# Rows of the next expert transposed between the two halves of the down products

## The chip, the cores and the metric

The kernel runs on one core of one Trainium2 chip. The metric is the device time of one launch in microseconds (us). Three runs of the kernel before took 445.80, 446.79 and 448.35 us; their median, 446.79 us, is the time before.

## The reference

One step of a one-layer streaming encoder, all in fp32: a prompt of 512 rows and a sample of 64 rows, each row 1024 wide. A pooling mixer and differential attention come first, then a layer of 16 experts, and a last RMSNorm. What matters here is the layer of experts: a router gives each row two of 16 experts with weights, and each expert works on its rows.

```python
h2 = rmsnorm(x, g_ffn)
for e in range(N_EXPERTS):                                   # 16
    he = jax.nn.silu(h2 @ w_gate[e]) * (h2 @ w_up[e])        # 1024 -> 256
    moe = moe + combine[..., e:e+1] * (he @ w_down[e])       # 256 -> 1024
x = x + moe
```

## The kernel before

The program is written engine by engine, with semaphores between them; the order of every queue is the order in which the code is written. The first 250 us or so are the projections, the attention, the pooling, the output projection and the router. Then 16 experts follow one another; each takes up to 128 rows (a program branch for rows beyond that stands at the end).

For expert i, by engine:

- POOL gathers the rows of expert i by indirect DMA into `xg[i % 2]` (`gather_h2`, three experts ahead). It waits for the list of rows (`idx_ready`) and for the transposes that free the buffer (`xg_transposed`). It also gathers the sums so far (`gather_acc`) and stores results.
- SP loads three matrices of 1 MB for each expert into a ring of four slots.
- PE (TensorE) does for expert i, in `expert`: 32 gate and up products with 128 x 128 weights (`gate_up`, L1183; the trace shows two records of MATMUL for each of them, 64 in all); then the eight transposes of the rows of expert i + 1 (`transpose_rows`, L1177) into PSUM banks 0 and 1; then the lists of rows of expert i + 3 (`lists_of`, L1242, five small products, L1174); then the down products of expert i - 1 in two halves of 512 columns (`down_split`, L1198), six products each: two by two for the high and low parts of the weights (L1204, L1205), and two with the low part of the activations (L1209). Each half raises `down_done`.
- ACT (ScalarE) does the silu of expert i (L1595) when the gate products end, then eight copies of 128 columns (`rows_out`, L1574) that take the transposed rows of expert i + 1 out of PSUM into `xT`, scaled by `g_ffn`. The last copy raises `xT_act`, for which the gate products of expert i + 1 wait (L1249). Then it makes the high part of the down weights of expert i + 1 (`wd_his`, L1576), which waits for both halves of the down products of expert i - 1. From expert 6 on it also sums squares (L1601).
- DVE (VectorE) makes the product of silu and up (`he_out`), reads out the lists (`lists_out`), adds the down products to the sums (`add_rows`) when both halves are done, and makes the low part of the down weights (`wd_los`).

Experts 0 to 3 and 12 to 15 are written out, experts 4 to 11 are a loop of two turns. The parts of ACT and DVE are written out in full. The rows of experts 0 and 1 reach `xT` partly by DVE (`xT_dve`), and expert 0 has no down products beside it. The functions that the change touches, and what calls them:

Of the kernel before, what the change touches and what calls it, by code (L numbers as in the profile page):

```python
# [29 lines left out]
ALU = mybir.AluOpType  # L30
# [57 lines left out]
def build(nc, x_prompt, x_sample, cache_k, cache_v, state_pool, g_mix, w_in, w_pool, pool_scale,  # L88
# [4 lines left out]
    with ctx:  # L93
# [253 lines left out]
        lam_exp = sem("lam_exp")  # L347
        lam_made = sem("lam_made")
        lam_spread = sem("lam_spread")
# [48 lines left out]
        xT_dve = sem("xT_dve")  # L398
        xT_act = sem("xT_act")
        up_full = sem("up_full")  # L400
        gact_ready = sem("gact_ready")
# [184 lines left out]
        def _(pool):  # L586
# [45 lines left out]

            pool.wait_ge(lam_made, 1)
            pool.partition_broadcast(neglam[:, :], lam_t[0:1, 6:7]).then_inc(lam_spread, 1)
# [171 lines left out]
        def _(pe):  # L806
# [375 lines left out]

            def gate_up(slot, b, signal):  # L1183
                for w, first in ((wg_sb[slot], 0), (wu_sb[slot], FC)):
                    for c in range(FC):
                        for k in range(KC):
                            ins = pe.matmul(ps[:, 2 + b, (first + c) * P:(first + c + 1) * P], w[:, k, c * P:(c + 1) * P],  # L1187
                                            xT[:, b, k, :], start=(k == 0), stop=(k == KC - 1))
                ins.then_inc(signal, 1)
# [7 lines left out]

            def down_split(u, i, bank):  # L1198

                b, w_hi = u % 2, wd_hi(i if isinstance(i, int) else u)  # L1200
                for half in range(2):
                    n = slice(half * 512, (half + 1) * 512)
                    for c in range(FC):
                        pe.matmul(ps[:, bank + half, :], he_hi[:, b, c, :], w_hi[:, c, n], start=(c == 0), stop=False)  # L1204
                        pe.matmul(ps[:, bank + half, :], he_hi[:, b, c, :], wd_lo[u][:, c, n], start=False, stop=False)  # L1205
                    if half == 0:
                        pe.wait_ge(he_lo_ready, i + 1)
                    for c in range(FC):
                        ins = pe.matmul(ps[:, bank + half, :], he_lo[:, b, c, :], w_hi[:, c, n], start=False, stop=(c == FC - 1))  # L1209
                    ins.then_inc(down_done, 1)  # L1210

            def first_rows():
# [23 lines left out]
            def expert(it, u, left):  # L1236
# [9 lines left out]

                if isinstance(it, int) and i <= 1:
                    pe.wait_ge(xT_dve, i + 1)
                pe.wait_ge(xT_act, i + 1)  # L1249
                pe.wait_ge(ring_loaded[u], it * 48 + 48)  # L1250
                gate_up(u, b, up_full)
                if isinstance(it, int) and i == 1:
                    for n in (1, 2):
                        lists_of(n)
                if left is None or left >= 1:
                    pe.wait_ge(xg_loaded[1 - b], it * (8 * RING) + 16 * ((u + 1) // 2 + 1))
                    transpose_rows(1 - b, xg_transposed)
                if first:
                    pe.wait_ge(tab_ready, 1)
                    for n in range(2):  # L1260
# [3 lines left out]
                if not first and left != 0:  # L1264
# [3 lines left out]
                    pe.wait_ge(wd_lo_ready, i)  # L1268
                    down_split((u - 1) % RING, i - 1, 4)
                if left == 1:  # L1270
# [45 lines left out]
        def _(act):  # L1316
# [287 lines left out]
            for i in range(E):  # L1604
# [5 lines left out]
                if i + 1 < E:  # L1610
                    act.wait_ge(xg_transposed, i + 2)
                    for k in range(4 if i == 0 else 0, KC):
                        ins = rows_out((i + 1) % 2, k)
                    ins.then_inc(xT_act, 1)
                    if i < E - 2:
# [28 lines left out]
        def _(dve):  # L1644
# [132 lines left out]
            step(dve.tensor_tensor(lam_t[:, 4:5], lam_t[:, 3:4], lam_t[:, 2:3], ALU.subtract))  # L1777
            dve.tensor_scalar(lam_t[:, 6:7], lam_t[:, 4:5], -LAMBDA_INIT, None, ALU.add).then_inc(lam_made, 1)
            w_in_los(3)
# [535 lines left out]
```

## Time and profile before

| | |
|---|---|
| three runs, median | 446.79 us (445.80 to 448.35) |
| the profiled execution, its own time | 445.62 us |
| its span, first to last instruction | 443.2 us |
| PE busy | 417.2 us (94%) |
| DVE, ACT, POOL busy | 273.6, 197.6, 125.0 us |
| mean granted TensorE clock | 0.985 |

The profile is of one execution. Start times count from the span's start. A record of a matmul overlaps the next one (they are pipelined), so distances of starts tell the pace, and the length of a single record does not. PEld is the weight load, which runs ahead of its matmul. The idle time in brackets is the engine's own just before the record, with what ended it.

### The profile page before, as it was taken

How to read it: one execution, taken by the hardware profiler on the slowest of the kernel's cores; microseconds unless marked ns; L12 is line 12 of the kernel's file. 1: busy time of each engine (PE TensorE's matmuls, PEld its weight loads, DVE VectorE, ACT ScalarE, POOL GpSimd, SP SyncE). 2: the span in 40 equal slices, each digit the busy share in tenths (PEclk: the TensorE clock that was granted, in tenths of full speed). 3: DMA queues.
4: the chain of work that ended last, by engine and by line, in shares of the span. 5: the costliest groups of instructions: out<-in, count | busy, mean ns of one | idle time of the engine just before them, and what ended most of it. 6: DMA issues, size and time to landing. Idle time of an engine off the chain costs nothing.

```text
span 443.2 us, 7774 instructions
## 1 busy us (share of the span) xinstructions
PE 417.2 (94%) x2926; PEld 365.2 (82%) x2927; DVE 273.6 (62%) x655; ACT 197.6 (45%) x485; POOL 125.0 (28%) x207
## 2 busy tenths in 40 slices
PE   7899999999999999999998998999999999999970
PEld 3786999997777777788895988999999999989950
DVE  3855231707779888464258897555577777569770
ACT  6475321605666755232124433444555555447340
POOL 2010000200143407250001304333345555355331
PEclk9999999999999999999998999999999999999995
DMA  8851705306000069814126599999999999973220
GB/s 280 295 164 48 226 1 167 130 1 198 2 1 3 1 266 378 328 53 163 78 95 247 172 405 389 363 363 352 362 352 361 355 350 382 351 274 129 57 78 21
DMA packets 32073, 91.36 MB, mean 206 GB/s; under 512 B 11200, under 2 KB 11712, under 8 KB 27942
## 3 DMA queue, kind: packets, MB, share of 16 engines
q1 hardware_dynamic: 20790, 71.97, 43.9%
q0 software_dynamic: 11248, 18.93, 12.0%
q8 instruction: 21, 0.34, 0.3%
q14 instruction: 14, 0.11, 0.1%
HBM read 86.38 MB, written 26.01 MB: 254 GB/s over the span
## 4 chain that ended last, share of the span: by engine, by line
PE 64%; DVE 16%; DMA 7%; issue 6%; ACT 4%; POOL 0%; POOLq 0%; SPq 0%; DVEq 0%; ACTq 0%
PE ps L1187 13%; PE ps L822 10%; PE ps L824 9%; PE ps L823 9%; DMA region_x<-h_rows,lists 5%; PE ps L978 2%; PE ps L1204 2%; PE ps L1205 2%; PE ps L1209 2%; PE ps L1124 2%; PE ps L943 2%; PE ps L1180 1%; DMA region_w<-in_w_in 1%; DMA out_y_sample<-region_x,lists 1%; PE ps L961 1%
## 5 line engine op out<-in xcount | busy, mean ns | idle before, releaser
L1187 PEld LDWEIGHTS ps<-region_p,region_a 128*128 128x128 f32 x512 | 58.3, 192 | 1.7 <-DVE region_p L2024 1.1
L1187 PE MATMUL ps<-region_p,region_a 128*128 128x128 f32 x512 | 58.5, 275 | 0.7 <-DVE region_p L2024 0.7
L824 PE MATMUL ps<-region_a_r,region_w_r 128*128 128x288 f32 x192 | 56.5, 294 | 0.0
L822 PE MATMUL ps<-region_a_r,ring_r 128*128 128x288 f32 x128 | 40.5, 317 | 0.0
L823 PE MATMUL ps<-region_a_r,ring_r 128*128 128x288 f32 x128 | 37.7, 295 | 0.0
L824 PEld LDWEIGHTS ps<-region_a_r,region_w_r 128*128 128x128 f32 x192 | 36.0, 188 | 0.0
L1574 ACT ACTIVATE region_p<-ps,gffn_sb 128x128 f32<-128x128 f32 x116 | 31.6, 383 | 8.5 <-PE ps L1180 6.7
L1595 ACT ACTIVATE region_t<-ps 128x256 f32<-128x256 f32 x16 | 6.1, 384 | 55.9 <-PE ps L1187 43.7
L699 POOL DMA_INDIRECT region_x<-h_rows,lists x13 | 16.6, 1280 | 48.6 <-DVE slot_w L2122 48.2
L1187 PEld LDWEIGHTS ps<-region_p,ring 128*128 128x128 f32 x256 | 29.1, 192 | 0.8 <-DVE region_p L2046 0.5
L1187 PE MATMUL ps<-region_p,ring 128*128 128x128 f32 x256 | 29.3, 275 | 0.4 <-DVE region_p L2046 0.4
L822 PEld LDWEIGHTS ps<-region_a_r,ring_r 128*128 128x128 f32 x128 | 24.0, 188 | 6.9 <-issue 3.3
L1187 PEld LDWEIGHTS ps<-region_p,region_w 128*128 128x128 f32 x256 | 29.2, 192 | 0.3
L1187 PE MATMUL ps<-region_p,region_w 128*128 128x128 f32 x256 | 29.2, 275 | 0.0
L1761 DVE TENSOR_SCALAR region_q<-ps 128x288 f32<-128x288 f32 x8 | 3.7, 458 | 39.8 <-PE ps L824 39.8
L2128 DVE TENSOR_TENSOR region_t_r<-region_t,ps 128x256 fp32r<-128x256 f32 x16 | 6.7, 419 | 33.8 <-ACT region_t L1595 24.3
L2145 DVE SCALAR_TENSOR_TENSOR mix<-ps,slot_w,mix 128x1024 f32<-128x1024 f32 x15 | 19.2, 1282 | 11.1 <-PE ps L1209 6.2
L823 PE MATMUL ps<-region_w_r,mix_r 128*128 128x512 f32 x64 | 25.0, 390 | 0.0
L1204 PE MATMUL ps<-region_q_r,region_t_r 128*128 128x512 f32 x60 | 24.7, 411 | 0.0
L823 PEld LDWEIGHTS ps<-region_a_r,ring_r 128*128 128x128 f32 x128 | 24.1, 188 | 0.0
L1437 ACT ACTIVATE region_p<-ps,negm 128x128 f32<-128x128 f32 (+4 forms) x40 | 20.7, 527 | 5.8 <-DVE negm L1793 5.8
L704 POOL DMA_INDIRECT out_y_prompt<-region_x,lists x12 | 12.0, 1002 | 35.8 <-DVE region_x L2161 32.7
(358 smaller groups left out, 1024.9 us busy)
## 6 DMA issues: line engine op xcount, KB each, us to landing
region_a<-in_w_gate SPq DMA_DIRECT2D x8, 1024.0 KB
region_a<-in_w_up SPq DMA_DIRECT2D x8, 1024.0 KB
region_a<-in_w_down SPq DMA_DIRECT2D x8, 1024.0 KB
region_w<-in_w_in SPq DMA_DIRECT2D x2, 2048.0 KB, 10.3
region_w<-in_w_out SPq DMA_DIRECT2D x2, 2048.0 KB, 8.0
ring<-in_w_gate SPq DMA_DIRECT2D x4, 1024.0 KB
ring<-in_w_up SPq DMA_DIRECT2D x4, 1024.0 KB
ring<-in_w_down SPq DMA_DIRECT2D x4, 1024.0 KB
```

The source lines that it names most:

```text
L699: pool.indirect_dma_start(out=dst, out_offset=None, in_=src, in_offset=bass.IndirectOffsetOnAxis(ap=at, axis=0), bounds_check=bound[n], oo ...
L704: pool.indirect_dma_start(out=dst, out_offset=bass.IndirectOffsetOnAxis(ap=at, axis=0), in_=src, in_offset=None, bounds_check=bound[n], oo ...
L822: pe.matmul(out, lhs_hi, rhs_hi, start=first, stop=False)
L823: pe.matmul(out, lhs_hi, rhs_lo, start=False, stop=False)
L824: return pe.matmul(out, lhs_lo, rhs_hi, start=False, stop=last)
L943: ins = pe.matmul(ps[:, b + c, 0:(t + 1) * P], q, kT[r, h, 0:(t + 1) * P], start=True, stop=True)
L978: ins = pe.matmul(ps[0:m, O_BANK[t], h * VD:(h + 1) * VD], aT[0:keys, n % 2, k * P:k * P + m], v, start=(k == 0), stop=(k == len(tiles) - 1))
L1187: ins = pe.matmul(ps[:, 2 + b, (first + c) * P:(first + c + 1) * P], w[:, k, c * P:(c + 1) * P], xT[:, b, k, :], start=(k == 0), stop=(k = ...
L1204: pe.matmul(ps[:, bank + half, :], he_hi[:, b, c, :], w_hi[:, c, n], start=(c == 0), stop=False)
L1437: ins = act.activation(prob[0:m, n % 2, c, 0:w], ps[0:m, 2 * (n % 2) + c, 0:w], ACT.Exp, bias=negm[0:m, n % 2, c:c + 1], scale=-1.0, accum ...
L1574: return act.activation(xT[:, b, k, :], ps[:, k // 4, (k % 4) * P:(k % 4 + 1) * P], ACT.Copy, scale=gffn_sb[:, k:k + 1])
L2145: dve.scalar_tensor_tensor(acc, ps[:, bank:bank + 2, :], slot_w[:, w:w + 1], acc, ALU.mult, ALU.add).then_inc(added, 1)
```

## The change

The transposes of the rows of expert i + 1 move from in front of the lists to between the two halves of the down products of expert i - 1 (for experts 1 to 14; expert 0, which has no down products, keeps its order). ACT's eight copies raise a new semaphore, `xT_half`, after the fourth, and `xT_act` after the eighth as before. From expert 2 on the gate products wait for `xT_half` at the first product, and for `xT_act` at the fifth (k = 4 of the first group of eight). The semaphore `lam_made` is dropped: its one signal goes to `lam_dots`, and its waiter on POOL waits for the second count of that.

```diff
@@ -345,7 +345,6 @@
         hist_evac = sem("hist_evac")
         lam_dots = sem("lam_dots")
         lam_exp = sem("lam_exp")
-        lam_made = sem("lam_made")
         lam_spread = sem("lam_spread")
         scores_full = sem("scores_full")
         negm_ready = sem("negm_ready")
@@ -397,6 +396,7 @@
         xg_transposed = sem("xg_transposed")
         xT_dve = sem("xT_dve")
         xT_act = sem("xT_act")
+        xT_half = sem("xT_half")
         up_full = sem("up_full")
         gact_ready = sem("gact_ready")
         he_ready = sem("he_ready")
@@ -630,7 +630,7 @@
                 pool.wait_ge(ktok_evac, t + 1)
                 pool.dma_start(kp_v[t] if t < PT else ks_v, k_st[0:rows(t), t, :]).then_inc(k_stored, 16)
 
-            pool.wait_ge(lam_made, 1)
+            pool.wait_ge(lam_dots, 2)
             pool.partition_broadcast(neglam[:, :], lam_t[0:1, 6:7]).then_inc(lam_spread, 1)
 
 
@@ -1180,10 +1180,12 @@
                     ins = pe.transpose(ps[:, k // 4, (k % 4) * P:(k % 4 + 1) * P], src[:, k, :], ident[:, :])
                 ins.then_inc(signal, 1)
 
-            def gate_up(slot, b, signal):
+            def gate_up(slot, b, signal, rest=None):
                 for w, first in ((wg_sb[slot], 0), (wu_sb[slot], FC)):
                     for c in range(FC):
                         for k in range(KC):
+                            if rest is not None and first == 0 and c == 0 and k == KC // 2:
+                                pe.wait_ge(xT_act, rest)
                             ins = pe.matmul(ps[:, 2 + b, (first + c) * P:(first + c + 1) * P], w[:, k, c * P:(c + 1) * P],
                                             xT[:, b, k, :], start=(k == 0), stop=(k == KC - 1))
                 ins.then_inc(signal, 1)
@@ -1195,7 +1197,7 @@
                                         start=(c == 0), stop=(c == FC - 1))
                 ins.then_inc(signal, 1)
 
-            def down_split(u, i, bank):
+            def down_split(u, i, bank, between=None):
 
                 b, w_hi = u % 2, wd_hi(i if isinstance(i, int) else u)
                 for half in range(2):
@@ -1208,6 +1210,8 @@
                     for c in range(FC):
                         ins = pe.matmul(ps[:, bank + half, :], he_lo[:, b, c, :], w_hi[:, c, n], start=False, stop=(c == FC - 1))
                     ins.then_inc(down_done, 1)
+                    if half == 0 and between is not None:
+                        between()
 
             def first_rows():
 
@@ -1244,18 +1248,24 @@
                     pe.wait_ge(idx_ready, i + n + EARLY + (1 if first and n == 0 else 0))
                     slot_lists((u + n) % RING * EPG + it + (u + n) // RING, (u + n) % RING)
 
-                if isinstance(it, int) and i <= 1:
+                early = isinstance(it, int) and i <= 1
+                if early:
                     pe.wait_ge(xT_dve, i + 1)
-                pe.wait_ge(xT_act, i + 1)
+                    pe.wait_ge(xT_act, i + 1)
+                else:
+                    pe.wait_ge(xT_half, i - 1)
                 pe.wait_ge(ring_loaded[u], it * 48 + 48)
-                gate_up(u, b, up_full)
+                gate_up(u, b, up_full, None if early else i + 1)
                 if isinstance(it, int) and i == 1:
                     for n in (1, 2):
                         lists_of(n)
-                if left is None or left >= 1:
+
+                def next_rows():
                     pe.wait_ge(xg_loaded[1 - b], it * (8 * RING) + 16 * ((u + 1) // 2 + 1))
                     transpose_rows(1 - b, xg_transposed)
+
                 if first:
+                    next_rows()
                     pe.wait_ge(tab_ready, 1)
                     for n in range(2):
                         lists_of(n)
@@ -1266,7 +1276,7 @@
                     if not (isinstance(it, int) and i == 1):
                         pe.wait_ge(added, i - 1)
                     pe.wait_ge(wd_lo_ready, i)
-                    down_split((u - 1) % RING, i - 1, 4)
+                    down_split((u - 1) % RING, i - 1, 4, next_rows)
                 if left == 1:
                     pe.wait_ge(idx_ready, E + EARLY + 1)
                     pe.wait_ge(he_ready, i + 1)
@@ -1611,6 +1621,8 @@
                     act.wait_ge(xg_transposed, i + 2)
                     for k in range(4 if i == 0 else 0, KC):
                         ins = rows_out((i + 1) % 2, k)
+                        if i >= 1 and k == KC // 2 - 1:
+                            ins.then_inc(xT_half, 1)
                     ins.then_inc(xT_act, 1)
                     if i < E - 2:
                         wd_his(i + 1)
@@ -1775,7 +1787,7 @@
             dve.tensor_copy(histT[:, :, :], ps[:, 3, 0:H * HIST].rearrange("p (g s) -> p g s", g=H)).then_inc(hist_evac, 1)
             dve.wait_ge(lam_exp, 1)
             step(dve.tensor_tensor(lam_t[:, 4:5], lam_t[:, 3:4], lam_t[:, 2:3], ALU.subtract))
-            dve.tensor_scalar(lam_t[:, 6:7], lam_t[:, 4:5], -LAMBDA_INIT, None, ALU.add).then_inc(lam_made, 1)
+            dve.tensor_scalar(lam_t[:, 6:7], lam_t[:, 4:5], -LAMBDA_INIT, None, ALU.add).then_inc(lam_dots, 1)
             w_in_los(3)
             for j in range(H + 1, 2 * H):
                 head_out(j)
```

On PE, expert 2's turn (the later turns repeat it), the order before, from the end of the gate products (L1187) over the transposes (L1180), the lists (L1174) and the first half of the down products (L1204, L1205, L1209):

```order
L1187 MATMUL ps<-region_p,region_a 128x128 x31
L1180 MATMUL ps<-ident,region_x 128x128 [waits xg_loaded1]
L1180 MATMUL ps<-ident,region_x 128x128 x7
L1174 MATMUL ps<-region_q,region_v 128x8 [waits idx_ready,onehot_ready]
L1174 MATMUL ps<-region_q,region_v 128x8 x4
L1204 MATMUL ps<-region_q_r,region_t_r 128x512 [waits wd_lo_ready,added,he_ready]
L1205 MATMUL ps<-region_a_r,region_t_r 128x512
L1204 MATMUL ps<-region_q_r,region_t_r 128x512
L1205 MATMUL ps<-region_a_r,region_t_r 128x512
L1209 MATMUL ps<-region_q_r,region_t_r 128x512 [waits he_lo_ready]
L1209 MATMUL ps<-region_q_r,region_t_r 128x512
```

and now, from the end of that first half (L1211 here) to the fifth gate product of the next expert (L1189):

```order
L1211 MATMUL ps<-region_q_r,region_t_r 128x512 [waits he_lo_ready]
L1211 MATMUL ps<-region_q_r,region_t_r 128x512
L1180 MATMUL ps<-ident,region_x 128x128 [waits xg_loaded1]
L1180 MATMUL ps<-ident,region_x 128x128 x7
L1206 MATMUL ps<-region_q_r,region_t_r 128x512
L1207 MATMUL ps<-region_a_r,region_t_r 128x512
L1206 MATMUL ps<-region_q_r,region_t_r 128x512
L1207 MATMUL ps<-region_a_r,region_t_r 128x512
L1211 MATMUL ps<-region_q_r,region_t_r 128x512 x2
L1189 MATMUL ps<-region_p,region_w 128x128 [waits ring_loaded3,xT_half]
L1189 MATMUL ps<-region_p,region_w 128x128 x3
L1189 MATMUL ps<-region_p,region_w 128x128 [waits xT_act]
```

The transposes stand behind six of the twelve down products instead of in front of all of them and of the lists; six products are left between them and the next expert's gate products, whose one wait has become two.

On PE, expert 1, the first with down products: before, the transposes stood ahead of the third group of lists, which waits for `idx_ready`.

```order
L1174 MATMUL ps<-region_q,region_v 128x8 [waits idx_ready,onehot_ready]
L1174 MATMUL ps<-region_q,region_v 128x8 x4
L1180 MATMUL ps<-ident,region_x 128x128 [waits xg_loaded0]
L1180 MATMUL ps<-ident,region_x 128x128 x7
L1174 MATMUL ps<-region_q,region_v 128x8 [waits idx_ready,onehot_ready]
L1174 MATMUL ps<-region_q,region_v 128x8 x4
L1204 MATMUL ps<-region_q_r,region_t_r 128x512 [waits wd_lo_ready,he_ready]
```

Now the lists and the first half come first.

```order
L1174 MATMUL ps<-region_q,region_v 128x8 [waits idx_ready,onehot_ready]
L1174 MATMUL ps<-region_q,region_v 128x8 x4
L1174 MATMUL ps<-region_q,region_v 128x8 [waits idx_ready,onehot_ready]
L1174 MATMUL ps<-region_q,region_v 128x8 x4
L1206 MATMUL ps<-region_q_r,region_t_r 128x512 [waits wd_lo_ready,he_ready]
L1207 MATMUL ps<-ring_r,region_t_r 128x512
L1206 MATMUL ps<-region_q_r,region_t_r 128x512
L1207 MATMUL ps<-ring_r,region_t_r 128x512
L1211 MATMUL ps<-region_q_r,region_t_r 128x512 [waits he_lo_ready]
L1211 MATMUL ps<-region_q_r,region_t_r 128x512
L1180 MATMUL ps<-ident,region_x 128x128 [waits xg_loaded0]
L1180 MATMUL ps<-ident,region_x 128x128 x7
```

The wait for `idx_ready` now has nothing of the transposes in front of it. The order of ACT's, DVE's and POOL's instructions is as before.

## Rows read from the trace of the kernel before

**Rows 1.** The page: busy time of PE and ACT, and the granted clock by slices.

```profile
PE 417.2 (94%) x2926; PEld 365.2 (82%) x2927; DVE 273.6 (62%) x655; ACT 197.6 (45%) x485; POOL 125.0 (28%) x207
...
PEclk9999999999999999999998999999999999999995
```

**Rows 2.** Stretches: length, busy of PE, PEld, DVE, ACT, POOL, granted clock, DMA share, GB/s.

```profile
304.50:315.50 11.00, 11.00 (x92) 10.49 (x91) 5.67 (x9) 4.55 (x11) 4.09 (x3) 1.00 0.95 363
...
381.50:393.60 12.10, 11.06 (x90) 10.37 (x90) 8.47 (x23) 5.55 (x13) 6.02 (x6) 1.00 0.85 332
```

**Rows 3.** Waits of PE over the whole span: total us, times, longest.

```profile
PE ps L1174 <- DVE slot_w L2122: 1.5, 1, 1.5
...
PE ps L1180 <- DMA region_x<-h_rows,lists: 1.0, 1, 1.0
```

**Rows 4.** The chain that ended last, in order of time: start, us.

```profile
368.70 20.81 DMA region_x<-h_rows,lists
389.56 1.09 PE ps L1180 x8
```

**Rows 5.** Timeline of PE and PEld, expert 5's turn: start, us, line.

```profile
311.50 1.04 PE L1180 MATMUL ps<-ident,region_x 128*128 128x128 f32 x8
...
312.37 0.27 PE L1174 MATMUL ps<-region_q,region_v 128*128 x5
...
312.50 0.47 PE L1204 MATMUL ps<-region_q_r,region_t_r 128*128 128x512 f32 x1
...
313.97 0.39 PE L1204 MATMUL ps<-region_q_r,region_t_r 128*128 128x512 f32 x1
...
315.11 7.34 PEld L1187 LDWEIGHTS ps<-region_p,region_a 128*128 128x128 f32 x64
315.34 7.30 PE L1187 MATMUL ps<-region_p,region_a 128*128 128x128 f32 x64
```

**Rows 6.** Timeline of ACT, same turn, cut after four copies, then whole.

```profile
312.57 1.14 ACT L1574 ACTIVATE region_p<-ps,gffn_sb 128x128 f32<-128x128 f32 x4 [0.49 <-PE ps L1180]
...
312.57 2.17 ACT L1574 ACTIVATE region_p<-ps,gffn_sb 128x128 f32<-128x128 f32 x8 [0.49 <-PE ps L1180]
315.59 1.99 ACT L1588 CAST region_q_r<-region_a 128x1024 fp32r<-128x1024 f32 x2 [0.84 <-PE ps L1209]
```

**Rows 7.** Timeline, a gate start after a wait (expert 1), its second record; a start without.

```profile
257.62 0.69 DVE L2024 TENSOR_TENSOR region_p<-ps,gffn_sb 128x512 f32<-128x512 f32 x1
...
258.36 0.38 PE L1187 MATMUL ps<-region_p,region_a 128*128 128x128 f32 x1 [0.65 <-DVE region_p L2024]
...
258.57 0.50 PE L1187 MATMUL ps<-region_p,region_a 128*128 128x128 f32 x3
...
315.44 0.39 PE L1187 MATMUL ps<-region_p,region_a 128*128 128x128 f32 x2
```

**Rows 8.** Timeline of PE, expert 1's turn.

```profile
265.86 1.07 PE L1180 MATMUL ps<-ident,region_x 128*128 128x128 f32 x8
268.41 0.27 PE L1174 MATMUL ps<-region_q,region_v 128*128 128x8 bf16 x5 [1.48 <-DVE slot_w L2122]
```

**Rows 9.** Timeline of DVE and POOL, the gather three experts ahead, expert 5's turn.

```profile
313.38 0.15 DVE L2122 TENSOR_REDUCE slot_w<-ps 128x1 f32<-128x3 f32 x1
...
313.80 1.33 POOL L699 DMA_INDIRECT region_x<-h_rows,lists  x1 [4.62 <-DVE slot_w L2122]
```

**Rows 10.** Timeline of DVE, the low part of the down weights, expert 7's turn.

```profile
340.31 2.35 DVE L2135 TENSOR_TENSOR ring_r<-ring,region_q_r 128x1024 fp32r<-128x1024 f32 x2
```

**Rows 11.** Timeline of PE: expert 12's gate, expert 14's turn, expert 15's gate.

```profile
381.22 7.30 PE L1187 MATMUL ps<-region_p,ring 128*128 128x128 f32 x64
...
411.34 1.04 PE L1180 MATMUL ps<-ident,region_x 128*128 128x128 f32 x8
...
417.67 2.50 PE L1187 MATMUL ps<-region_p,region_w 128*128 128x128 f32 x21
```

**Rows 12.** The page's group of ACT's copies: count, busy us, mean ns of one.

```profile
L1574 ACT ACTIVATE region_p<-ps,gffn_sb 128x128 f32<-128x128 f32 x116 | 31.6, 383 | 8.5 <-PE ps L1180 6.7
```

## Prediction

> **What bounds the kernel now.** I read the page first: PE is busy for 417.2 of 443.2 us, and its granted clock is full in nearly every slice [rows 1]. Then the stretches: from 271 us on each expert takes one turn of 11.0 us in which PE has no idle time at all, while DMA is 0.95 busy and ACT only 4.55 us [rows 2]. So in the expert stage anything put on PE, or any wait of PE, is paid in full; work of ACT is free as long as PE doesn't wait for it. The waits of PE name two of interest: 1.5 us for the lists in expert 1's turn and 1.0 us for gathered rows [rows 3]. The chain shows the second: a gather issued at 368.70 landed 20.81 us later, and the transposes started at 389.56 [rows 4]. Expert 12's gate products had started at 381.22 [rows 11]; in an undisturbed turn the transposes follow a gate's start after 7.14 us (64 records, 0.11 us apart, 7.30 us with the last one's tail [rows 5]), so they were wanted at 388.36. This late gather costs 1.20 us, which the turn of 12.10 us confirms [rows 2]. It is all that the move of the transposes can win in this execution.
>
> **What the move does in an ordinary turn.** Transposes, lists and down products take the same time in another order. In [rows 5] the eight transposes take 312.37 - 311.50 = 0.87 us, the lists 0.13, the first half 313.97 - 312.50 = 1.47 and the second half 315.34 - 313.97 = 1.37. Before, ACT's copies had the lists and both halves as cover, 2.97 us. Now they have the second half alone, 1.37 us.
>
> Count from S, the start of the transposes. The gate products of the next expert are wanted at S + 0.87 + 1.37 = S + 2.24. ACT starts copying at S + 1.07 (312.57 against 311.50), has four copies at + 1.14 and eight at + 2.17 [rows 6]; ACT is idle before the copies in this row, so nothing in its queue makes them later. The two signals thus fall at S + 2.21 and S + 3.24. From a signal to PE takes 0.05 us: DVE ends at 258.31 and the waiting matmul starts at 258.36 [rows 7].
>
> - First product: possible at S + 2.26, wanted at S + 2.24. But its weight load otherwise runs 0.23 us ahead, under the last down product (315.11 against 315.34 [rows 5]), and can't before the signal. A gate that starts from a wait has its second record 0.21 us after the first (258.57), one that doesn't 0.10 (315.44) [rows 7]. So 0.02 + 0.11 = 0.13 us are lost.
> - Fifth product, the ninth record: wanted 8 x 0.111 = 0.89 us after the first, at S + 3.13; possible at S + 3.29, thus 0.16 late, and 0.11 for the load that isn't ahead: 0.27 us. The first loss is inside this one, since PE would get there at S + 3.26, still before the signal.
>
> So each gate start loses **0.27 us**. This holds for experts 2 to 14, 13 of them; expert 15's gate has expert 14's down products in front too (transposes at 411.34, gate at 417.67 [rows 11]) and waits for nothing. 13 x 0.27 = 3.5 us. Bounds: 13 x 0.16 = 2.1 if the late load costs nothing, 13 x (0.13 + 0.27) = 5.2 if the two losses add.
>
> **A price by the Trainium skill.** By the Trainium skill (ScalarE: Activation LUTs, Rules for kernel authors) an ACTIVATE costs about 0.3 us and 0.83 ns for each element, an estimate of 0.41 us for 128 columns and 3.25 for eight; each gate would wait 1.08 us more, and my forecast would become 463 us. The trace disagrees: eight of them end in 2.17 us [rows 6].
>
> **Expert 1's turn.** PE reached the end of its lists at 265.86, did the transposes, and then stood until 268.41 for the lists from DVE [rows 8]; the 0.87 us of transposes lay in that wait. Now the wait comes first and is ended by the same DVE record, and the transposes come behind it, uncovered: **+0.87 us**. The gate loss after it is among the 13.
>
> **The late gather.** The gather three experts ahead is issued 0.27 us after the lists are read out (313.38 + 0.15, then 313.80 [rows 9]), but POOL also waits for the transposes that free the buffer. These now start 0.13 + 1.47 = 1.60 us later, are seen done at S + 1.07 = 314.17, and the gather goes out at 314.2 to 314.4, some 0.5 us later than now. It is wanted 1.60 us later, and two gate losses (0.54) lie between. The time left from issue to need grows from 388.36 - 368.70 = 19.66 us to 21.3; it took 20.8 to land. So the wait should go: **-1.20 us**, and the weights, which share the DMA engines, get 2% longer turns. Its bounds are 0 and -1.20 in this execution.
>
> **What costs nothing.** ACT makes the next down weights' high part behind the copies, now from S + 3.24, 1.0 us after the gate was due instead of 0.25 [rows 5, 6]. It takes 2.0 us, so both parts stand 3.0 us after the gate's start. DVE begins the low part at 340.31 [rows 10], 3.0 us after that turn's gate (two turns of 11.0 us after 315.34), and needs one part at a time. That cover is a whole turn deep, since PE wants the result a turn later. The end of the second half, which frees weights for SP and sums for DVE, keeps its place. `lam_made` into `lam_dots` moves one signal between the same two instructions: 0. The register instructions for the added wait run ahead on PE's sequencer: 0, at most hundredths in the loop.
>
> **The sum.** 445.62 (the profiled execution) + 0.87 + 3.5 - 1.20 = 448.8 us. This execution lies 1.17 us under the median of the three runs, 446.79, and no row tells what the others lose. I carry half of that, 0.6, over: **449.4 us**.
>
> **The rivals.** About 0.5%, 2.2 us, is what a measurement of this kernel can tell: faster is below 444.6, slower above 449.0.
>
> 1. *Late gathers cost more in ordinary runs.* The three runs spread over 2.55 us while PE's work is fixed, and DMA is near full [rows 2], so gathers are what can differ. If all of the 1.17 us is theirs, the change takes 2.4 us away; with the lower bound of the gate loss, 446.79 + 0.87 + 2.1 - 2.4 = 447.4 us. Against it: the profile has one late gather in 13 turns. Within 0.5%.
> 2. *The gates don't wait.* The second half of the down products hides the copies after all; it decides whether the signals reach PE before S + 2.01 and S + 3.02, some 0.25 us earlier than I find. Then 445.62 + 0.87 - 1.20 = 445.3 us, and if expert 1's transposes find another cover, 444.4. For it: the margin is a quarter of a microsecond, and the ends of records are modelled for matmuls. Against it: ACT's start 1.07 us behind the first transpose is measured, and so are its copies.
> 3. *Both losses add, and the gather stays late*, since it is issued later too: 445.62 + 0.87 + 5.2 + 0.6 = 452.3 us.
> 4. *The copies don't overlap.* One takes 383 ns [rows 12]; end to end eight take 3.06 us instead of 2.17, and 13 gates lose 0.89 more: 461 us. In the trace they overlap in every turn. The Trainium skill's price above would be a case of this.
>
> That the change does not do what it says can be left out: the order of PE's queue shows both waits and the new place.
>
> **How the numbers follow.** My case 0.54 (0.49 slower, 0.05 within); rival 1 0.20, within; rival 2 0.14 (0.06 within, 0.08 faster); rival 3 0.08 and rival 4 0.02, slower; anything else that makes it faster 0.02. Together: faster 0.10, within 0.5% 0.31, slower 0.59. The range goes from rival 1 with a little of rival 2, 446.8, to just under rival 3, 452.0. My case alone has 447.4 (2.1 for the gates, median not carried) to 451.1 (5.2, half carried).
>
> **What would show it.** In the changed profile: turns of 11.25 to 11.30 us instead of 11.0, with 0.2 to 0.3 us of idle time of PE at the first and fifth gate product, ended by ACT's copies (L1584); the second ACT group of a turn starting 1.0 us after the gate's due time; no wait for gathered rows at expert 12; expert 1's gate to expert 2's gate longer by 0.9 to 1.2 us. Turns of 11.0 us would prove the gate loss wrong, and turns above 11.5 us would mean the copies come later than S + 1.07. If a wait for gathered rows stays, the 1.20 us are wrong.

## The result: 450.29 against 446.76 us

The changed kernel takes 450.29 us (median of 20 runs, 447.75 to 451.89), the kernel before 446.76 (20 runs, 445.15 to 448.38): a ratio of 1.008, interval 1.0065 to 1.0095. It is slower, by more than the 0.5% that the prediction set as its bound. (Ratios here and below are those on record with their 95% intervals; they can differ by up to 0.15% from the quotient of the two medians beside them.) The forecast was 449.4, the range 446.8 to 452.0.

The profiled execution took 450.57 us, with a span of 448.7. The page's busy times of it answer to [rows 1]; PE has 4.8 us more and still the same share:

```profile
PE 422.0 (94%) x2926; PEld 365.6 (81%) x2927; DVE 274.1 (61%) x655; ACT 196.2 (44%) x485; POOL 119.1 (27%) x207
```

The waits of PE (first line) and of its weight loads (second line) over the whole span, us in total, times and longest, answer to [rows 3]:

```profile
PE ps L1174 <- DVE slot_w L2134: 2.4, 1, 2.4
...
PEld ps L1189 <- ACT region_p L1584: 3.0, 11, 0.3
```

The wait for the lists has grown from 1.5 to 2.4 us, the wait for gathered rows is not in the answer any more, and weight loads of the gate products now wait for ACT's copies, 0.3 us at most.

Expert 5's turn in the timeline (start, us, instruction, idle time before it and what ended it) answers to [rows 5, 6, 9]:

```profile
317.51 1.03 PE L1180 MATMUL ps<-ident,region_x 128*128 128x128 f32 x8
318.30 0.48 PE L1206 MATMUL ps<-region_q_r,region_t_r 128*128 128x512 f32 x1
318.58 2.17 ACT L1584 ACTIVATE region_p<-ps,gffn_sb 128x128 f32<-128x128 f32 x8 [2.08 <-PE ps L1180]
319.30 0.99 POOL L699 DMA_INDIRECT region_x<-h_rows,lists  x1 [6.67 <-PE ps L1180]
319.77 6.35 PEld L1189 LDWEIGHTS ps<-region_p,region_a 128*128 128x128 f32 x55 [0.28 <-ACT region_p L1584]
319.77 7.55 PE L1189 MATMUL ps<-region_p,region_a 128*128 128x128 f32 x64
320.60 2.04 ACT L1598 CAST region_q_r<-region_a 128x1024 fp32r<-128x1024 f32 x2
320.81 0.19 PEld L1189 LDWEIGHTS ps<-region_p,region_a 128*128 128x128 f32 x1
328.76 1.04 PE L1180 MATMUL ps<-ident,region_x 128*128 128x128 f32 x8
```

With S = 317.51, the start of the transposes, the copies start at S + 1.07 and take 2.17 us as before, the first gate load goes at S + 2.26 and the fifth product's (the one at 320.81) at S + 3.30. The 64 gate records take 7.55 us instead of 7.30: the loss appears as longer records, not as idle time of PE. From S to the next S it is 11.25 us.

Where the 5.5 us between the two spans (443.2 and 448.7 us) went, by the first gate record of an expert (expert 1 and expert 15, the same products as in [rows 7, 11]):

| | expert 1's gate | expert 15's gate | between | from there to the end |
|---|---|---|---|---|
| before | 258.36 | 417.67 | 159.31 | 25.55 |
| after | 260.85 | 423.32 | 162.47 | 25.38 |

So 3.16 us arose between these two gates, 2.49 before expert 1, and -0.17 behind. (The executions' own times differ by 4.95 us; 0.5 us less of the later one lies outside the span.) The three terms of the sum, 0.87 + 3.5 - 1.20, make 3.17.

### The profile page after: what moved, and what is told of

It reads as the page before. It is cut to its first block, busy times and chain, and to the rows that moved or that the text cites. A ratio compares the mean times of both kernels' runs of the same rounds, so it can differ in the third digit from the quotient of the medians.

```text
span 448.7 us, 7774 instructions
## 1 busy us (share of the span) xinstructions
PE 422.0 (94%) x2926; PEld 365.6 (81%) x2927; DVE 274.1 (61%) x655; ACT 196.2 (44%) x485; POOL 119.1 (27%) x207
## 4 chain that ended last, share of the span: by engine, by line
PE 79%; DVE 10%; ACT 4%; issue 3%; DMA 1%; POOLq 0%; POOL 0%; SPq 0%; DVEq 0%; ACTq 0%
PE ps L1189 23%; PE ps L822 10%; PE ps L824 9%; PE ps L823 9%; PE ps L1206 3%; PE ps L1207 3%; PE ps L1211 3%; PE ps L1180 3%; PE ps L978 2%; PE ps L1124 2%; PE ps L943 2%; DMA region_x<-in_x_prompt 1%; PE ps L961 1%; PE ps L1111 1%; PE ps L818 1%
## 5 line engine op out<-in xcount | busy, mean ns | idle before, releaser
L1189 PEld LDWEIGHTS ps<-region_p,region_a 128*128 128x128 f32 x512 | 58.3, 192 | 3.5 <-ACT region_p L1584 1.9
L1189 PE MATMUL ps<-region_p,region_a 128*128 128x128 f32 x512 | 60.3, 278 | 0.7 <-DVE region_p L2036 0.7
L699 POOL DMA_INDIRECT region_x<-h_rows,lists x13 | 12.9, 995 | 66.0 <-PE ps L1180 51.5
L1189 PEld LDWEIGHTS ps<-region_p,ring 128*128 128x128 f32 x256 | 29.1, 192 | 1.6 <-issue 0.7
L1189 PE MATMUL ps<-region_p,ring 128*128 128x128 f32 x256 | 29.9, 278 | 0.4 <-DVE region_p L2058 0.4
L1189 PEld LDWEIGHTS ps<-region_p,region_w 128*128 128x128 f32 x256 | 29.2, 192 | 1.1 <-ACT region_p L1584 0.8
L1189 PE MATMUL ps<-region_p,region_w 128*128 128x128 f32 x256 | 30.0, 277 | 0.0
L1206 PE MATMUL ps<-region_q_r,region_t_r 128*128 128x512 f32 x60 | 25.9, 432 | 0.0
L2157 DVE SCALAR_TENSOR_TENSOR mix<-ps,slot_w,mix 128x1024 f32<-128x1024 f32 x15 | 19.2, 1281 | 10.5 <-PE ps L1211 7.1
L1447 ACT ACTIVATE region_p<-ps,negm 128x128 f32<-128x128 f32 (+4 forms) x40 | 20.7, 527 | 5.8 <-DVE negm L1805 5.8
L1542 ACT ACTIVATE region_v<-region_q 128x512 f32<-128x512 f32 (+1 forms) x10 | 6.3, 627 | 32.7 <-DVE region_q L1912 19.5
```

What stands on the lines that cost most here:

```text
L699: pool.indirect_dma_start(out=dst, out_offset=None, in_=src, in_offset=bass.IndirectOffsetOnAxis(ap=at, axis=0), bounds_check=bound[n], oo ...
L1447: ins = act.activation(prob[0:m, n % 2, c, 0:w], ps[0:m, 2 * (n % 2) + c, 0:w], ACT.Exp, bias=negm[0:m, n % 2, c:c + 1], scale=-1.0, accum ...
L2157: dve.scalar_tensor_tensor(acc, ps[:, bank:bank + 2, :], slot_w[:, w:w + 1], acc, ALU.mult, ALU.add).then_inc(added, 1)
```

## The experiments

The theory: each ordinary turn loses 0.27 us because ACT's copies lost 1.6 us of their cover, expert 1's turn loses 0.87 us of transposes that lay in a wait, and 1.20 us of a late gather come back. The rivals that matter now: the second wait costs by itself, the turns are longer for another cause, and the gather was punctual by chance.

"Stage" below is the time from expert 1's first gate record to expert 15's, 159.31 before and 162.47 with the change.

### Both signals, transposes at their old place

```diff
-                if first:
+                if left is None or left >= 1:
                     next_rows()
+                if first:
...
-                    down_split((u - 1) % RING, i - 1, 4, next_rows)
+                    down_split((u - 1) % RING, i - 1, 4)
```

> The transposes go back in front of the lists, in every turn; the two signals and the two waits of the gate products stay. Theory (the gate products wait because the copies have too little cover behind the transposes): with the lists and both halves as cover again, neither wait is ever open, turns are 11.0 us, and the time is that of the kernel before, 446.8 +- 0.7 us, ratio 1.000. Rival (the added wait itself, its instructions in PE's queue or the weight load it holds back, costs the 0.27 us a turn): turns stay at 11.25 us, and the time is 446.8 + 13 x 0.27 = 450.3 us, ratio 1.008.

Measured: 446.37 against 446.81 us, ratio 0.9996 (0.9975 to 1.0017); stage 158.91. Turns are 10.98 us and no weight load waits for ACT's copies. The wait for rows is here too. PE's timeline, two ordinary turns and expert 12's:

```profile
312.57 1.04 PE L1180 MATMUL ps<-ident,region_x 128*128 128x128 f32 x8
...
323.55 1.04 PE L1180 MATMUL ps<-ident,region_x 128*128 128x128 f32 x8
...
390.25 0.98 PE L1180 MATMUL ps<-ident,region_x 128*128 128x128 f32 x7 [0.66 <-DMA region_x<-h_rows,lists]
```

Two signals in place of one cost nothing as long as both are early, so the whole loss of the ordinary turns comes with the place; and the late gather returns with the old place.

### The new place with one signal

```diff
...
-                    pe.wait_ge(xT_half, i - 1)
+                    pe.wait_ge(xT_act, i + 1)
                 pe.wait_ge(ring_loaded[u], it * 48 + 48)
-                gate_up(u, b, up_full, None if early else i + 1)
+                gate_up(u, b, up_full)
...
```

Left out above: `xT_half` itself and ACT's raising of it, which go too.

> The transposes stay between the halves; the gate products wait once, at the first product, for all eight copies. Theory: the first product can start 3.24 + 0.05 us after the first transpose, is wanted at 2.24, and its load costs 0.11 more, so a turn loses 1.16 us instead of 0.27: turns of 12.1 us, and 450.3 + 13 x 0.89 = 461.9 us, ratio 1.034. Rival (the loss of 0.27 us is that of transposes amid the down products, not of waits for the copies): turns of 11.25 us and 450.3 us, ratio 1.008.

Measured: 460.46 against 446.81 (461.9 was forecast), ratio 1.031 (1.0281 to 1.0339); stage 175.71, turns of 12.14 us. The waits of PE, and one gate of its timeline:

```profile
PE ps L1188 <- ACT region_p L1583: 11.6, 13, 1.0
...
322.35 0.82 PE L1188 MATMUL ps<-region_p,region_a 128*128 128x128 f32 x5 [0.89 <-ACT region_p L1583]
```

All 13 gates wait for the eighth copy, 0.9 us in the mean. This is the predicted mechanism without its remedy: the cover of 1.37 us against copies that stand at S + 3.24. The split signal gets 0.9 us of each 1.16 back. The turn of expert 1 showed something else, told further down.

### The change, with expert 1's transposes at their old place

```diff
-                if first:
+                if early:
                     next_rows()
+                if first:
...
-                    down_split((u - 1) % RING, i - 1, 4, next_rows)
+                    down_split((u - 1) % RING, i - 1, 4, None if early else next_rows)
```

> As the change, but in expert 1's turn the transposes stand where they stood before, ahead of the lists for which PE waits there. Theory: the 0.87 us of expert 1's transposes are hidden in that wait again, and expert 2's gate does not wait (0.27): 450.3 - 1.14 = 449.2 us, ratio 1.005; the later turns stay at 11.25 us. Rival (that stretch is paced by DVE, and PE's order there is worth nothing): 450.3 us, and expert 2's gate starts as late as in the change.

Measured: 448.33 against 446.81 (449.2 was forecast), ratio 1.0045 (1.0026 to 1.0064); stage 161.39, 1.08 less than with the whole change. The timelines of PE, the changed kernel first:

```profile
260.85 1.38 PE L1189 MATMUL ps<-region_p,region_a 128*128 128x128 f32 x10 [0.66 <-DVE region_p L2036]
...
270.89 0.27 PE L1174 MATMUL ps<-region_q,region_v 128*128 128x8 bf16 x5 [2.40 <-DVE slot_w L2134]
272.49 1.04 PE L1180 MATMUL ps<-ident,region_x 128*128 128x128 f32 x8
274.76 0.49 PE L1189 MATMUL ps<-region_p,region_a 128*128 128x128 f32 x2
```

and this one:

```profile
259.21 7.41 PE L1189 MATMUL ps<-region_p,region_a 128*128 128x128 f32 x64 [0.67 <-DVE region_p L2037]
...
266.71 1.07 PE L1180 MATMUL ps<-ident,region_x 128*128 128x128 f32 x8
269.26 0.27 PE L1174 MATMUL ps<-region_q,region_v 128*128 128x8 bf16 x5 [1.48 <-DVE slot_w L2135]
272.25 0.94 PE L1189 MATMUL ps<-region_p,region_a 128*128 128x128 f32 x7
```

From gate to gate, expert 1's turn is 13.91 us with the change (274.76 - 260.85) and 13.04 here (272.25 - 259.21), as before the change: 0.87 us. With the gate loss of expert 2, which goes too, 1.14 were expected of the stage. By the two ratios this kernel is 1.6 us below the change, with intervals wide enough for 1.1.

### Transposes behind four of the twelve down products

```diff
                     if half == 0:
+                        if between is not None:
+                            between()
                         pe.wait_ge(he_lo_ready, i + 1)
...
-                    if half == 0 and between is not None:
-                        between()
```

> As the change, but the transposes stand behind four of the twelve down products instead of six, so that eight of them cover the copies: 0.87 + 8 x 0.228 = 2.69 us from the first transpose to the gate instead of 2.24. Theory: the first load is wanted at 2.46, the signal reaches it at 2.26; the fifth is wanted at 3.47, its signal is there at 3.29; no gate waits, turns are 11.0 us, and the time is 450.3 - 3.5 = 446.8 us, ratio 1.000; expert 1's 0.87 us stay, and the late gather of expert 12's turn comes back at most in part, since the transposes stand 1.1 us later than before. Rival (transposes amid the down products cost 0.27 us a turn wherever they stand): 450.3 us, ratio 1.008, turns of 11.25 us.

Measured: 446.65 against 446.81 (446.8 was forecast), ratio 0.9999 (0.9985 to 1.0013). Eight products now cover the copies, and the turns are 11.0 us; the gate loss is gone. But the stage is 160.89, for expert 1's turn took 15.5 us. Stretches of this kernel (length, busy of PE, PEld, DVE, ACT and POOL, granted clock, DMA share, GB/s), the first two in that turn:

```profile
265.00:269.31 4.31, 1.91 (x25) 1.60 (x24) 3.97 (x20) 0.38 (x1) 0.99 (x1) 1.00 1.01 414
269.31:272.72 3.41, 3.41 (x13) 2.93 (x12) 0.61 (x1) 2.17 (x8) 0.98 (x1) 0.50 1.01 424
273.26:284.26 11.00, 11.00 (x90) 10.44 (x89) 5.66 (x9) 4.02 (x10) 3.17 (x3) 1.00 0.88 323
```

For 3.41 us the granted clock was 0.50, the 1.2 GHz level. PE had stood 2.40 us for the lists until 267.81. The third stretch is an ordinary turn. The gathered rows only just came in time; the waits of the weight loads have them twice:

```profile
PEld ps L1180 <- DMA region_x<-h_rows,lists: 0.6, 2, 0.4
```

At expert 12 PE lost next to nothing by it, at expert 13 the transposes started about 0.1 us late.

### Both edits together

The diffs of the last two kernels (expert 1's transposes at their old place, and four of the twelve down products in front of the others) in one: the later place, without the gate loss and without the loss of expert 1's turn.

> The two edits together: transposes behind four of the twelve down products from expert 2 on, and in expert 1's turn where they stood before. Theory: no gate waits (3.5 us back), expert 1's 0.87 us are hidden again, and PE does not stand for 2.4 us in one piece in that turn, after which two of four profiles with the transposes behind the lists show a granted clock of 0.50 for 3.4 us (some 1.5 us, in about half of the executions: 0.8): 450.3 - 3.5 - 0.87 - 0.8 = 445.1 us, ratio 0.996, turns of 11.0 us, no clock of 0.50 in expert 1's turn. Rival (the gains overlap, since DVE paces that stretch): 446.6 us as with four products alone, ratio 1.000.

Measured: 445.94 against 445.95, ratio 0.9999 (0.9981 to 1.0018); stage 159.36, nothing gained. Turns are 11.0 us and expert 1's is 13.01, as wanted. The 0.87 and 3.5 us should be gone, and with the gather's 1.20 kept the stage should be 158.1 us (159.31 - 1.20). The missing part is in the turn from expert 13's gate to expert 14's, 11.96 us long (10.76 before), in the timelines of PE and DVE:

```profile
393.76 7.30 PE L1189 MATMUL ps<-region_p,region_a 128*128 128x128 f32 x64
...
399.98 1.28 DVE L2158 SCALAR_TENSOR_TENSOR mix<-ps,slot_w,mix 128x1024 f32<-128x1024 f32 x1 [2.92 <-DMA mix<-summed_rows,lists]
401.36 0.47 PE L1206 MATMUL ps<-region_q_r,region_t_r 128*128 128x512 f32 x1 [0.30 <-issue]
402.94 1.09 PE L1180 MATMUL ps<-ident,region_x 128*128 128x128 f32 x8 [0.41 <-DMA region_x<-h_rows,lists]
...
405.72 7.31 PE L1189 MATMUL ps<-region_p,region_a 128*128 128x128 f32 x64
```

PE stood 0.41 us for gathered rows here, and 0.30 us just before that because of gathered sums: DVE waited 2.92 us for them, and the down products, which need DVE's result, started 0.1 us after it. (The profile names no releaser for this wait, it says "issue"; the cause is read from the times.) By starts the two delays are longer than the idle time, since a record's tail covers part of it: the down products start 7.60 us after the gate, against 7.07 in the same turn of the kernel with four products. So the later place alone doesn't make the gathers punctual.

### Half of the copies on DVE

```diff
-                    for k in range(4 if i == 0 else 0, KC):
+                    for k in range(4, KC):
...
+                if i >= 1:
+                    dve.wait_ge(xg_transposed, i + 2)
+                    rows_out((i + 1) % 2).then_inc(xT_dve, 1)
```

The gate products' first wait is for `xT_dve` instead of `xT_half`; place and expert 1 as in the kernel with expert 1's transposes at their old place.

> Transposes between the halves as in the change (in expert 1's turn where they stood before), but DVE copies the first four blocks in one instruction of 0.69 us while ACT copies the last four in 1.14 us. Theory: the first product's rows are ready 1.2 + 0.69 = 1.9 us after the first transpose, its load is wanted at 2.01; ACT's are ready at 2.21, wanted at 2.9. So no gate waits though the transposes stand where the change put them, turns are 11.0 us, the late gather is gone, and the time is 445.1 us, ratio 0.996. Rival (the place between the halves costs in itself): turns of 11.25 us, 448.3 us as with expert 1 put back alone. A third outcome: DVE is held up by its own queue in the later turns and the gates wait for it, turns above 11.0 us from expert 6 on.

Measured: 446.20 against 445.95, ratio 1.001 (0.9988 to 1.0032); stage 160.28. Again the ordinary turns are 11.0 us, so the place between the halves costs nothing by itself; and again gathers come late, rows in expert 12's turn and sums in expert 13's, by the timelines of PE and DVE:

```profile
390.46 1.09 PE L1179 MATMUL ps<-ident,region_x 128*128 128x128 f32 x8 [0.38 <-DMA region_x<-h_rows,lists]
...
399.44 1.28 DVE L2153 SCALAR_TENSOR_TENSOR mix<-ps,slot_w,mix 128x1024 f32<-128x1024 f32 x1 [3.09 <-DMA mix<-summed_rows,lists]
400.83 0.47 PE L1205 MATMUL ps<-region_q_r,region_t_r 128*128 128x512 f32 x1 [0.74 <-issue]
```

A second way to remove the gate loss ends as the first: this kernel and the one with both edits were each forecast at 445.1 us, which takes the late gather to be gone, and both missed that.

### Longer turns at the old place

The kernel before, with one spare product in front of each gate from expert 2 on; the output doesn't depend on it.

```diff
                 pe.wait_ge(ring_loaded[u], it * 48 + 48)
+                if not (isinstance(it, int) and i <= 1):
+                    keep_running(1, 2 + b)
                 gate_up(u, b, up_full)
```

> The kernel before, order and waits untouched, with one spare product of 512 columns (0.215 us) in front of each expert's gate products from expert 2 on; it is no part of the result. Turns become 11.2 us, as long as the change's but for 0.05. Question: what took the late gather away in the changed kernel. Theory of the prediction (the later place of the transposes, 1.6 us more until the rows are wanted): here the place is the old one, so PE still waits for gathered rows at expert 12, 0.5 us or more, and the time is 446.0 + 14 x 0.215 - at most 0.7 = 448.3 to 449.0 us. Rival (longer turns let the DMA engines, 0.95 busy, catch up, and any slack on PE's side is eaten by them): no wait for gathered rows on PE, and 446.0 + 3.0 - 1.0 = 448.0 us or less.

Measured: 447.64 against 446.25, ratio 1.0029 (1.0008 to 1.005); stage 161.91, turns of 11.2 us. PE's timeline:

```profile
402.71 1.09 PE L1180 MATMUL ps<-ident,region_x 128*128 128x128 f32 x8 [0.51 <-DMA region_x<-h_rows,lists]
```

Longer turns alone push the wait one expert later and shrink it to 0.51 us, but don't remove it. Neither expectation came out as written: the time is the rival's (448.0 or less), but the wait that the rival excluded is there; the theory has the wait, but at expert 12 and with 448.3 us or more.

### Spare products in expert 1's wait, twice, beside the change again

To keep PE busy in the wait after which the clock had fallen: the changed kernel and ten spare products of 512 columns, whose results nobody reads.

```diff
                 if isinstance(it, int) and i == 1:
                     for n in (1, 2):
                         lists_of(n)
+                    keep_running(10, 4)
```

> As the change, but in expert 1's turn PE runs ten spare products of 512 columns (2.15 us at full clock) into an unused bank after the second group of lists, where it would otherwise stand for 2.4 us. They are no part of the result. Theory (that idle stretch lets the granted clock fall to 0.50 in about half of the executions, which costs some 1.5 us each time): no clock of 0.50 there, and 450.3 - 0.8 = 449.5 us, ratio 1.006. Rival (the clock there is worth nothing in the mean, and the change costs 3.5 us by its waits and expert 1's transposes alone): 450.3 us, ratio 1.008. If the spare products run into the signal, expert 2's gate starts later than 13.9 us after expert 1's.

> The changed kernel once more, beside the next one on the same chip, for a second profile. Theory (PE's idle 2.4 us in expert 1's turn lets the granted clock fall in some executions): 450 us, ratio 1.008; turns of 11.25 us; a clock of 0.50 in expert 1's turn as likely as not. Rival: never a clock of 0.50 there with this order.

> The kernel with the spare products in expert 1's wait, beside the changed kernel on the same chip. Theory: no clock of 0.50 in expert 1's turn, 0.5 to 0.8 us less than the changed kernel in the median. Rival: the same time as the changed kernel within 0.3 us.

Measured: 449.07 (ratio 1.0073, 1.0045 to 1.01) and again 449.32 (1.0076, 1.0047 to 1.0106); the changed kernel beside the second, 449.55 (1.0089, 1.0056 to 1.0122). Their stages are 162.47, 162.55 and 162.52. The products filled the wait, by PE's timeline of the first of them:

```profile
266.86 2.32 PE L880 MATMUL ps<-ones 128*128 128x512 bf16 x10
269.40 0.27 PE L1174 MATMUL ps<-region_q,region_v 128*128 128x8 bf16 x5 [0.23 <-DVE slot_w L2135]
```

The intervals overlap, and the stretch over expert 1's turn of the changed kernel's second profile has the full clock:

```profile
268.00:274.90 6.90, 4.49 (x39) 3.69 (x37) 4.74 (x20) 1.54 (x6) 1.43 (x2) 1.00 1.00 421
```

So the low clock in expert 1's turn is no main part of the change's loss. Whether it takes some tenths of the median stays open. The count "two of four" in an expectation above was one profile too high when it was written; with this profile it is right: of four profiles with 2.4 us of idle time there, two fell to 0.50 and two, both of the changed kernel itself, did not.

## Why the prediction was right

- **What the move does in an ordinary turn** held to a hundredth. The signals were to reach the first load at S + 2.26 and the fifth product's at S + 3.29; the records say S + 2.26 and S + 3.30, and the turn is 11.25 us. The cause was the copies' cover: with two signals and the old place nothing was lost, with eight products as cover, or half of the copies on DVE, the turns went back to 11.0. "Idle time of PE at the first and fifth gate product" was not to be seen as such: PE has no such wait in its list. It is the weight load of the first product that stood for ACT, 0.28 us by the row of 319.77; at the fifth, too little to be listed, and what is lost lies in the longer records.
- **Expert 1's turn** held: 0.87 us, measured by undoing that part alone.
- **The late gather** held in what came of it: no wait for rows in the two profiles of the change, the two with spare products and the one with expert 1 undone, and turns of 11.25 and 11.04 us around expert 12. Its working was 0.6 us off. These are, in the changed kernel, the gather that expert 12's turn needs and the transposes that need it:

```profile
375.58 1.00 POOL L699 DMA_INDIRECT region_x<-h_rows,lists  x1 [3.13 <-PE ps L1180]
...
396.26 0.93 PE L1180 MATMUL ps<-ident,region_x 128*128 128x128 f32 x7
```

  From issue to need are 20.7 us, not 21.3, because POOL issues the gather at S + 1.8 (319.30 for S = 317.51 above) and not at S + 1.1 to 1.3. With the 20.8 us of [rows 4] it would still have been 0.1 late; it landed after 20.0. The same two times in all profiles with turns of 11.0 to 11.25 us, for the same expert's rows (us; where PE waited, the need is when it would have started):

| | issue to need | issue to landing |
|---|---|---|
| before; both signals at the old place | 19.7; 19.7 | 20.8; 20.4 |
| longer turns at the old place | 20.1 | 19.7 |
| four products; both edits; half on DVE | 20.2; 20.2; 20.2 | 20.1; 19.8; 20.7 |
| the change, twice | 20.7; 20.7 | 20.0; 20.4 |
| with spare products, twice; expert 1 undone | 20.7; 20.7; 20.7 | 19.2; 19.9; 19.4 |

  The left column is the prediction's mechanism: the later place gives 0.5 us, and two gate losses give 0.5 more. The right column varies by 1.6 us from profile to profile, and no row tells why. So the five punctual gathers follow from the place and the gate losses together, but with margins of 0.3 to 1.5 us against that variation there was luck in it that none was late. The kernels without the loss had a wait for rows of 0.4 us (both edits at expert 13, half on DVE at expert 12) or a start just in time (four products). The 1.20 us thus came back in full only in kernels that had the gate loss.
- **What costs nothing** held. The casts started at 320.60, 0.85 us after the gate was due (1.0 forecast), and no gate waited for weights.
- **The sum** came to 448.8 for an execution like the one profiled before; the one profiled after had 450.57. The weak step is "I carry half of that, 0.6, over". No row said that the change gives the other half back, and it did not: the medians differ by 3.53 us, the terms make 3.17, and added to the whole median they would have given 446.79 + 3.17 = 450.0 us. What differed between the two executions beside the terms arose in the first 20 us: expert 0's gate starts at 250.58 instead of 248.09, which is 2.49 us, as much as at expert 1's. Stretches of both from 13.20 to 16.50, the changed kernel first:

```profile
13.20:16.50 3.30, 3.30 (x12) 2.71 (x12) 0.89 (x3) 0.00 (x0) 0.00 (x0) 0.50 0.89 323
```

```profile
13.20:16.50 3.30, 3.30 (x20) 2.87 (x19) 1.49 (x4) 2.07 (x4) 0.00 (x0) 1.00 0.97 301
```

  The clock was at half in the one and full in the other, with 12 records of PE instead of 20. Ahead of that the one was late by 0.88 us, by the timelines, again the changed kernel first:

```profile
11.19 0.73 PE L835 MATMUL ps<-mix_r,region_a_r 128*128 128x512 f32 x2 [1.13 <-ACT region_a_r L1356]
```

```profile
10.31 0.73 PE L835 MATMUL ps<-mix_r,region_a_r 128*128 128x512 f32 x2 [0.20 <-ACT region_a_r L1346]
```

  The second profile of the change has this low clock too, at 13.57 to 16.98, though the order of PE's instructions there is as before the change; no other profile has it, and as long a wait at this line (1.3 us with both edits together) went without. Whether that is chance stays open. Against its being in most runs of the change speaks that these were only 0.23 us above the kernel with spare products, in whose profile expert 0's gate started 1.43 us earlier (249.27 against 250.70).
- **The rivals.** *Late gathers cost more in ordinary runs* fell: no gather was late in the changed kernel's profiles, and the loss was over 0.5%. *The gates don't wait* fell: they do, in each turn. *Both losses add, and the gather stays late* fell on both points. *The copies don't overlap* fell: eight take 2.17 us again, and with it the 463 us that came of adding up eight whole prices of the Trainium skill (ScalarE: Activation LUTs, Rules for kernel authors).

No version beat the kernel before by a measurable amount.

## What to carry to other kernels

When a producer is moved later in an engine's queue, count from its end to its consumer what is left as cover for the engine between them; here 1.37 us of cover against 2.17 us of copies, and a signal in two parts paid for most of the gap but not all. A wait that work was hidden in is a resource: before moving that work, look where the wait will stand. And when a second resource is nearly full, a gain on the first may depend on the first being slow: undo the loss and see whether the gain stays. A forecast that hangs on half a microsecond between two times of 20 needs the spread of both, and one profile doesn't give it.

## What the runs showed of the hardware

- After PE had stood idle for 2.40 to 2.42 us in expert 1's turn, the granted clock was 0.50 for 3.4 us in two of four profiles. One of them stands above; the other is the new place with one signal:

```profile
267.26:270.68 3.42, 3.35 (x14) 2.70 (x15) 2.14 (x8) 0.00 (x0) 0.99 (x1) 0.50 1.01 424
```

  It cost about 1.6 us: expert 1's turn was 15.5 us in the kernel with four products, against 13.9 with the change, whose clock stayed at 1.00. After 1.5 us of idle time in the same place, in the six profiles with the transposes ahead, and with the wait filled, in two, it stayed at 1.00. What tells the two kinds of profile with 2.4 us apart was not found, and that the idle time is the cause is not shown. A stretch of this length at 0.50 also stands ahead of the experts, between 238 and 246 us, in ten of the twelve profiles, before the change and after (the two without are the new place with one signal and half of the copies on DVE). Spans therefore differ by more than the experts' turns, which is why the stage is compared above. In the changed kernel:

```profile
241.85:245.26 3.41, 3.41 (x14) 1.34 (x14) 2.86 (x17) 3.39 (x2) 1.47 (x2) 0.50 0.94 377
```

- How long a gather takes is no constant of this kernel: with the change, at turns of 11.25 us, it took 9.2 us from issue to landing in expert 5's turn and 20.0 in expert 10's. With turns of 12.14 us (the new place with one signal) none issued in the turns of experts 3 to 12 took more than 9.6. That the weight loads on the same DMA engines (0.95 busy [rows 2]) make the difference is likely, but not shown. At about 20 us, a quarter of a microsecond a turn on PE bears on whether it is waited for, as the table above shows.
